# Order of the first loads, and the first norm spread over three engines, in a hybrid decoder step

## The reference

```
def rmsnorm(x, g):
    y = x * rsqrt(mean(x * x, -1) + EPS)
    return y * g

def lru_mixer(xn, h0, conv_past, w_in, conv_w, conv_b, w_a, b_a, w_x, b_x, lam, w_out):
    gate, xb = split(xn @ w_in, 2)
    xc, tail = causal_dwconv(xb, conv_past, conv_w, conv_b)      # 4 taps
    r = sigmoid(block_diag(xc, w_a, b_a)); i = sigmoid(block_diag(xc, w_x, b_x))
    log_a = -8 * r * softplus(-lam); a = exp(log_a)
    h_t = a_t * h_{t-1} + sqrt(1 - a_t^2) * (i_t * xc_t)         # scan over time
    return (gelu(gate) * h) @ w_out
```

## Time and profile before

| | |
|---|---|
| median of 3 runs | 1723.23 us |
| lowest, highest | 1722.24, 1784.59 us |
| profiled execution | 1724.49 us |
| its span, slowest core (core 1) | 1722.9 us |
| spans of cores 0 to 7 | 1713.9, 1722.9, 1720.0, 1720.3, 1715.7, 1714.3, 1714.9, 1717.6 us |
| TensorE busy, core 1 | 1649.8 us (96%) |
| VectorE, ScalarE, GpSimd busy | 1260.4, 944.3, 571.1 us |
| TensorE idle before matmuls, sum | 64.9 us |

### The profile page before, as it was taken

The page is one execution under the profiler, slowest core; times in us unless marked ns, Lnnn a source line. Parts: engine busy times, 40 slices in busy tenths (PEclk is TensorE's granted clock), DMA queues, the critical chain, the costliest instruction groups (busy, mean ns, idle before and its releaser), DMA issues.

```text
span 1722.9 us, 35656 instructions; the slowest of 8 cores (1713.9 to 1722.9 us)
## 1 busy us (share of the span) xinstructions
PE 1649.8 (96%) x10895; PEld 1052.7 (61%) x10895; DVE 1260.4 (73%) x2654; ACT 944.3 (55%) x1895; POOL 571.1 (33%) x1046
## 2 busy tenths in 40 slices
PE   5899999999999999999989999899999999999996
PEld 3566666556666666666555556566666666666654
DVE  4766696987777676777757767888776767777786
ACT  4877779644444444456655444764444444565756
POOL 1143454322111111136864443802111111254543
PEclk9999999999999999999999999999999999999998
DMA  8710040073212121110085000224330303001112
GB/s 161 176 49 2 1 80 1 6 152 61 48 27 45 31 46 29 32 32 1 11 152 94 1 1 17 33 43 80 65 75 1 74 2 74 1 6 39 39 49 102
DMA packets 24218, 83.49 MB, mean 48 GB/s; under 512 B 1888, under 2 KB 15520, under 8 KB 18272
## 3 DMA queue, kind: packets, MB, share of 16 engines
q0 software_dynamic: 9712, 59.16, 19.5%
q1 hardware_dynamic: 13344, 20.84, 3.6%
q10 hardware_dynamic: 976, 1.21, 0.2%
HBM read 130.33 MB, written 10.03 MB: 81 GB/s over the span
## 4 chain that ended last, share of the span: by engine, by line
PE 78%; DMA 6%; DVE 5%; ACT 4%; issue 4%; POOL 2%; DVEq 0%; ACTq 0%; SPq 0%; POOLq 0%
PE PS L583 78%; DVE SB L567 4%; DMA SB<-xT 2%; ACT SB L531 2%; POOL SB L542 2%; ACT L531 1%; DVE SB L542 1%; DMA SB<-lru_w_g_in 1%; DMA SB<-st_fc 1%; DMA SB<-lru_w_out 1%; ACT PS L531 1%; DMA SB<-lru_w_x_in 0%; ACT SB L572 0%; DVE SB L574 0%; DVEq L293 0%
## 5 line engine op out<-in xcount | busy, mean ns | idle before, releaser
L583 PE MATMUL PS<-SB 128*128 128x352 bf16 (+7 forms) x10895 | 1649.8, 313 | 64.9 <-ACT SB L531 26.1
L583 PEld LDWEIGHTS PS<-SB 128*128 128x128 bf16 x10895 | 1052.7, 98 | 661.8 <-issue 107.0
L567 DVE SCALAR_TENSOR_TENSOR SB<-SB 128x352 f32<-128x352 f32 (+1 forms) x708 | 392.2, 573 | 220.9 <-ACT SB L572 192.4
L542 DVE TENSOR_TENSOR SB<-SB,PS 128x352 f32<-128x352 f32 (+3 forms) x968 | 462.0, 511 | 61.2 <-PE PS L583 41.4
L542 POOL TENSOR_TENSOR SB<-SB 128x352 f32<-128x352 f32 (+10 forms) x414 | 372.6, 913 | 310.5 <-DVE SB L567 119.3
L531 ACT ACTIVATE SB<-PS,SB 128x352 f32<-128x352 f32 (+1 forms) x432 | 256.8, 615 | 351.0 <-PE PS L583 336.1
L531 ACT ACTIVATE SB<-SB 128x352 f32<-128x352 f32 (+5 forms) x662 | 317.0, 504 | 229.8 <-DVE SB L567 137.6
L574 POOL COPY SB<-SB 128x2 f32<-128x2 f32 (+2 forms) x456 | 142.1, 317 | 646.7 <-ACT SB L572 464.6
L567 DVE SCALAR_TENSOR_TENSOR SB<-SB,PS 128x352 bf16<-128x352 f32 (+6 forms) x448 | 223.3, 547 | 92.6 <-ACT PS L531 49.9
L531 ACT ACTIVATE SB<-PS 128x352 f32<-128x352 f32 (+8 forms) x234 | 107.7, 471 | 116.3 <-PE PS L583 86.4
L572 ACT ACTIVATE SB<-PS 128x352 f32<-128x352 f32 (+2 forms) x376 | 152.8, 420 | 21.6 <-PE PS L583 8.9
(11 more groups left out here) (28 smaller groups left out, 73.0 us busy)
## 6 DMA issues: line engine op xcount, KB each, us to landing
SB<-ffn_w_up POOLq DMA_DIRECT2D x24, 1024.0 KB, 10.2
SB<-ffn_w_down POOLq DMA_DIRECT2D x12, 1024.0 KB, 8.8
SB<-xT SPq DMA_DIRECT2D x10, 704.0 KB, 9.6
yT<-SB SPq DMA_DIRECT2D x10, 704.0 KB, 3.3
SB<-ple_w_gate POOLq DMA_DIRECT2D x2, 2048.0 KB, 17.5
SB<-gm_w_in POOLq DMA_DIRECT2D x2, 2048.0 KB, 21.1
SB<-lru_w_x_in POOLq DMA_DIRECT2D x4, 512.0 KB, 10.6
SB<-lru_w_g_in POOLq DMA_DIRECT2D x2, 1024.0 KB, 20.2
```

The costliest lines, as they stand in the source:

```text
L542: emit(eng, lambda e: e.tensor_tensor(out=out.ap, in0=a.ap, in1=b.ap, op=op), R=[a, b], W=[out], cost=c)
L567: emit("dve", lambda e: e.scalar_tensor_tensor(out=out.ap, in0=a.ap, scalar=sa, in1=b.ap, op0=op0, op1=op1), R=rr, W=[out], cost=c)
L583: emit("pe", lambda e: e.matmul(ps.ap, lhsT=lhsT.ap, rhs=rhs.ap, start=start, stop=stop), R=[lhsT, rhs], W=[ps], cost=max(0.05, 0.000427 * ...
```

## The change

Four edits:

1. The four quarters of x tile 0 are issued first, ahead of `vecs`, and block 0 of `lw_x` waits for the first quarter (in place of block 1 for the second).
2. x tile 1 waits for block 2 of `lw_x` in place of block 1.
3. The norm of tile 0: squares of even chunks on ScalarE, of odd ones on VectorE (all eight were on ScalarE). The reciprocal root is written to an SBUF tile. For chunks 5, 6 and 7 GpSimd multiplies x by the gain beforehand (three one-operand instructions) and then by the root (three two-operand ones); VectorE keeps chunks 0 to 4.
4. `exp_step` of tile 0: even chunks go to GpSimd, odd ones stay on VectorE. The squares of tile 2's norm: odd chunks go to GpSimd, even ones stay on VectorE.

```
-        def norm(c0, n, gname, outs, sqs=None, sqeng="act", after=None, banks=BN, order=None, done=None):
+        def norm(c0, n, gname, outs, sqs=None, sqeng="act", after=None, banks=BN, order=None, done=None, pre=None):
...
             act(ps, ps, AF.Ln, bias=epsT.all(), order=[] if order is None else order())
-            last = act(ps, ps, AF.Exp, scale=-0.5)
+            r = ps if pre is None else pre[0]
+            last = act(r, ps, AF.Exp, scale=-0.5)
             if done is not None:
                 done(last)
             yield
+            if pre is not None:
+                for c, t in pre[1].items():
+                    ts(t, hv(c, c0, n), vcol(gname, c), ALU.mult, eng="pool")
             for c in range(KC):
-                stt(outs[c], hv(c, c0, n), vcol(gname, c), ps, ALU.mult, ALU.mult)
+                if pre is not None and c in pre[1]:
+                    tt(outs[c], pre[1][c], r, ALU.mult, eng="pool")
+                else:
+                    stt(outs[c], hv(c, c0, n), vcol(gname, c), r, ALU.mult, ALU.mult)
...
+        load_x(0, 4)
         load("act", VEC.all(), vecs, K("vec"))
-        load_x(0, 4)
         load("act", idf.all(), cst[:, 0:128], K("idf"))
         for q in range(4):
-            load("pool", lw_x.v(q), kp(w_lx_in[q], KC), K("lwx%d" % q), hblock(2, 4, 0, TN) if q == 1 else None)
-        load_x(1, 2, lw_x.v(1))
+            load("pool", lw_x.v(q), kp(w_lx_in[q], KC), K("lwx%d" % q), hblock(0, 2, 0, TN) if q == 0 else None)
+        load_x(1, 2, lw_x.v(2))
...
             return norm(c0, n, "nm0", [xn.v(c, (0, n)) for c in range(KC)], None, sqeng,
+                        pre=(a2m[0].v((0, n)), {c: thi[c].v((0, n)) for c in (5, 6, 7)}) if ti == 0 else None,
                         order=(lambda: phase("exp")) if phased else None, done=lambda op: keep("rstd", op))
...
-            eng = "dve" if ti == 0 or ti == 5 and c % 2 else "pool"
+            eng = "dve" if ti in (0, 5) and c % 2 else "pool"
...
-        for _ in lru_norm(0, "act"):
+        for _ in lru_norm(0, ["act", "dve"] * 4):
...
-                bg.append(("lru2", lru_norm(2, "dve", False)))
+                bg.append(("lru2", lru_norm(2, ["dve", "pool"] * 4, False)))
```

## The result

The changed kernel takes 1726.85 us (median of 14 runs) beside 1722.25 for the kernel before (14 runs), a ratio of 1.0026 with a 95% interval of [1.0018, 1.0034]: 4.6 us slower, where 3.7 faster was forecast, and 0.85 above the upper end of the range.

What follows compares the result with a forecast made beforehand. TensorE, 96% busy on slowest core 1, was taken as the bound, its start held by the load chain to lw_i. Loads -3.7, norm 0, exp_step and tile 2's squares 0: 1723.23 - 3.7 = 1719.5 us, range 1714 to 1726.

Steps and rivals of the forecast that it cites:

- The rate of x tile 0: Start of loading: x tile 0 alone flows at 357 GB/s and is in at about 6.3 us.
- The hole: Loads in 12 to 16 us, at 70 GB/s in place of 157: 2.2 us lost, gone after the change.
- same bytes, same arrival: Rival on the loads: lw_i has the same bytes ahead, so gain 0 to 1, time 1722.7; chance 0.20.
- Edit 2 at 1.3 us of mixing and landing: x tile 1 behind block 2: 1.3 us allowed for mixing and landing, its first half in at 24.0.
- The start of the projection: TensorE's first projection waits for block 0, landing at 12.4 us, and starts at 12 to 13.
- Edit 3 at nothing: Norm of tile 0: results ready at 12.8 us, 1.3 earlier than on one engine; worth 0 within the wait for lw_i.
- the cover: TensorE's wait for lw_i, 3.9 us after the change against 3.7 before, hides changes in tile 0's norm.
- 5 to 9 us in hand: Cores like core 5, with a smaller shift from the loads, have this much span to spare against the slowest.
- Edit 4 at nothing: exp_step and tile 2's squares: ScalarE sets the pace and GpSimd can hold the added 5.0 us, so worth 0.
- GpSimd becomes a bound: Rival: GpSimd's 5.0 us of squares and clamps delay tile 1's small copies and ScalarE; time 1724.5, chance 0.13.
- The clock at nothing: TensorE's clock stays at 1.00 through the wait for lw_i of 3.9 us; charged 0.
- The range: 1714 to 1726: from 1717.4 less 3 for the scheduler's new order, to 1724.5 and a little noise.

Runs made afterwards that it cites:

- f3: Kernel before with only exp_step of tile 0 and tile 2's squares half on GpSimd: no ratio, mean span of cores 0 to 3 -1.2 ± 0.6 us.
- h3: Kernel before with both load-order edits, and exp_step of tile 0 and tile 2's squares half on GpSimd: ratio 1.0005 [0.9994, 1.0016].
- f0: The kernel before, unchanged, profiled once more on another chip: its 484th matmul starts at 105.1 us, against 102.7 in the first profile.
- i2: Kernel before with both load-order edits and the first norm's squares split over ScalarE and VectorE: ratio 1.0016 [1.0007, 1.0026].
- g3: Changed kernel with all eight results of tile 0's norm on VectorE, root still in SBUF: too few times for a ratio; eight results took 4.06 us.
- h1: Kernel before with only the two load-order edits: ratio 0.9999 [0.9989, 1.0009], mean of the spans -0.5 ± 0.4 us.

## Why the prediction was wrong, step by step

- **The rate of x tile 0 (wrong, the first step that failed).** "At the rates of unmixed stretches" took 357 GB/s, measured in 26 to 28 us, for a stretch in which all eight cores begin. Core 3 had 142, 100, 285 and 303, core 1 in the mean of 2 to 12 us 220. The first quarter landed at 7.9 on core 3 (5 assumed), block 0 at about 16.8 (12.4 assumed). The 2.9 us that the sum took for mixing in 2 to 12 were no cost of mixing: with x tile 0 first, the cores write 195 GB/s in the mean there, against 198 mixed. The hole was not gone either: 38 GB/s in 10 to 12 on core 3, where x tile 0 had landed before the blocks flowed. This was the rival *same bytes, same arrival*, with its own argument, and 0.20 was too little for it: block 3 landed at 24.9 in the mean, at 25.1 before. The Trainium skill ("DMA: Bandwidth & Descriptors", on issuing engines not being separate DMA queues) says that transfers of all issuing engines run on the same 16 DMA engines and interleave, and that issuing on several engines saves only the time of the issue. Of their order, which the prediction puts beside it, the page says nothing; the 195 and 198 here show that it brought none. `lw_a` was to be issued at 24.5 and went at 29.1 in the mean, 31.6 on core 3.
- **Edit 2 at 1.3 us of mixing and landing (wrong).** x tile 1 now waits for block 2, which lands at 24 on core 3, and its first half takes 7.0 from there (28.6 in the mean, 24.0 forecast). Alone the edit gave +1.2 ± 0.7, no gain.
- **The start of the projection (half right).** It moved by 1.6 in the mean and not by 4.4; on core 3 block 0 ended last, as said, but late.
- **Edit 3 at nothing (wrong, the most costly).** The results were to take 2.7 us, at 0.50 and 0.91 each, as if each engine were alone; together they are 0.92 and 1.20 and stretch over 4.6, more than the 4.02 of eight on VectorE. So the split is a loss in itself and not a gain to be covered. The 0.91 was moreover no duration alone but the mean of 1.06 beside VectorE and 0.77 without it: the trace of before had shown the effect. The page of the Trainium skill that the prediction names for GpSimd's speed, "GPSIMD Engine Reference", says in its Specifications that the two contend; the prediction weighed its figure for speed and passed over that line. The second fault is the cover. The 3.7 us of wait for weights were core 1's. Core 5 had none, which the prediction saw, and in the mean the eight cores of before waited 1.1 for `lw_a` and `lw_i` together. The "5 to 9 us in hand" of the other cores were no property of these cores: each core's span scatters by 8 to 10 us from run to run, so every core can become the slowest. What covers a cost has to cover it on each of them.
- **Edit 4 at nothing (right in the sum, wrong in its reason).** The stretch of tile 2's squares was not one "where GpSimd is idle": clamps, squares and the small copies meet at 58 to 63. The rival *GpSimd becomes a bound* named the place to the row (ScalarE behind an L574 copy). Its price was about a third of the 5.0 (1.5 to 2.0 us between the 226th and the 246th matmul), and in f3 and h3 even this was given back.
- **The clock at nothing (wrong for the load order).** In the profile of before no core fell in 30 to 50 us, and from this the prediction charged nothing, though it forecast as long a wait behind an earlier start. Three to five cores of eight fell to 0.50 where edit 1 came without edit 3's delay. In the changed kernel it was one, three and four in three profiles. There is a misreading to avoid in the earlier trace rows as well. The 1.00 of its first rows is no reading: the trace of core 1 has no record of the clock before 22.5 us, and none of before's eight cores has one before 22.4. What the matmuls did there is in these two rows of core 1 before, columns as in the earlier trace rows:

```profile
20.50:22.50 2.00, 2.00 (x9) 0.99 (x7) 1.56 (x10) 0.47 (x1) 0.00 (x0) 1.00 0.89 164
23.00:25.00 2.00, 2.00 (x16) 1.28 (x14) 1.35 (x9) 1.23 (x3) 0.00 (x0) 1.00 1.00 192
```

  Both show TensorE busy throughout, with 9 and 16 matmuls; they start 0.29 us apart in the first and 0.15 in the second. In 68 to 70, where the record says 0.50, there were 9 too. So the projection begins at the lower level, in both kernels, until 23.5 before and 23.1 after in the mean.
- **The range.** Its upper end was 1724.5 plus noise. It added no term for two parts failing together, the load gain at zero and edit 3 at a price: 1722.25 plus the 4.7 of edit 3 alone is just above it.

Still open: where the rest of edit 3's 4.7 us arises. Beside the profile of before its single profile shows 2.1 by the 484th matmul, of which 1.2 are in the first eight matmuls, and 1.3 more behind it, in no place that I could name; beside f0 it shows none by the 484th. Open too are why edit 3 on top of the loads costs 1.9 and alone 4.7, and why the slowest core of i2 is 3.0 later.

## What to carry to other kernels

Work moved to GpSimd has two prices, its own and what it adds to VectorE's instructions beside it; where both engines read two operands from SBUF, add the times as if one engine did both. An operand moved from PSUM to SBUF so that GpSimd can read it can bring this about by itself. A stretch in which all cores begin loading has a rate of its own, to be read from that stretch over all cores, and reordering shares it out anew without adding to it. A wait that covers an edit has to be looked up on every core, and an earlier start in front of the same late arrival is only a longer wait, behind which TensorE may be granted half its clock.

## What the runs showed of the hardware

- A VectorE `scalar_tensor_tensor` of 128x352 (f32 to bf16, both tensors in SBUF) takes 0.51 us with GpSimd idle (g3) and 0.92, in the mean of five, beside GpSimd's two-operand instructions, which go from 0.77 to 1.09 to 1.20 each. With one of its tensors in PSUM it takes 0.51 beside GpSimd too (before, core 1, 79.89). GpSimd's one-operand instruction went from 0.48 to 1.19 while VectorE made diagonals.
- Before TensorE's first clock record (22.4 to 26.1 us on the cores of before) the profile's page and the rows by stretch show a clock of 1.00, while matmuls of 352 columns start 0.29 us apart, as they do at 0.50; at a recorded 1.00 they start 0.15 apart.
- With x tile 0 first on the queues, the cores part into two kinds, 174 to 180 and 204 to 220 GB/s over 2 to 12 us (after: cores 0, 3, 4, 7 and 1, 2, 5, 6), where a mixed start gave all of them 189 to 206. The mean hardly changes (195 and 198).
- In h1 core 3's clock fell to 0.50 (1.2 GHz) at 39.9 us, inside the second of its two waits for weights, after TensorE had been idle 2.4 of 3.8 us, and stayed there for 6.8 us; the changed kernel's core 3, idle 4.7 of 8.0 us there, kept 1.00.
